# Two mixture-of-experts layers on one core: an order of experts chosen on chip, with two blocks each for the last two

## The reference

```python
grp = argmax(x @ w_group + b_group)
e_logits = (x @ w_router + b_router).reshape(t, 4, 8)[grp]
top_p, top_i = lax.top_k(softmax(e_logits), 2)
eid = grp * 8 + top_i                         # 1024 assignments
y = (silu(xs @ w1[e]) * (xs @ w3[e])) @ w2[e] # for the tokens xs of each expert e
out = sum over a token's two experts of y * its weight
```

## Time and profile before

| what | value |
|---|---|
| median of 3 runs | 2249.36 us (2246.14 to 2252.11) |
| the profiled execution | 2244.45 us, its span 2242.6 us |
| granted TensorE clock, mean | 0.959 |
| busy PE, DVE, ACT, POOL | 88%, 36%, 18%, 6% |
| moved by DMA | 440.67 MB |

### The profile page before, as it was taken

One profiled execution on the slowest core, in us unless ns is written; L12 is line 12 of the kernel. 1 busy time (PEld: TensorE's weight loads), 2 busy tenths in 40 slices (PEclk: granted clock), 3 DMA queues, 4 the chain that ended last, 5 costly groups with the idle time before them and its releaser, 6 DMA issues. The chain is left out here.

```text
span 2242.6 us, 22709 instructions
## 1 busy us (share of the span) xinstructions
PE 1968.3 (88%) x8452; PEld 1080.9 (48%) x8452; DVE 800.1 (36%) x1497; ACT 392.8 (18%) x676; POOL 135.3 (6%) x136
## 2 busy tenths in 40 slices
PE   7999998877784999999999999999988977877782
PEld 4553335544443565666557776666554322322220
DVE  3426524312115355555554554323243111111015
ACT  2335531000002123222211011111020000000000
POOL 0001010311110000000000000000002101101000
PEclk9999998999997999999999999999989999999996
DMA  8402103699977211111011115222339999999993
GB/s 230 153 33 88 56 1 151 244 420 418 418 324 226 66 47 56 47 56 43 19 65 65 64 46 159 75 75 75 131 132 391 425 427 425 421 422 424 421 404 118
DMA packets 169830, 440.67 MB, mean 197 GB/s; under 512 B 25549, under 2 KB 129741, under 8 KB 143660
## 3 DMA queue, kind: packets, MB, share of 16 engines
q1 hardware_dynamic: 159084, 423.81, 49.5%
q0 software_dynamic: 10560, 16.08, 2.0%
q10 hardware_dynamic: 128, 0.02, 0.0%
HBM read 434.21 MB, written 24.22 MB: 204 GB/s over the span
## 5 line engine op out<-in xcount | busy, mean ns | idle before, releaser
L1431 PE MATMUL bank<-stream,work 128*64 128x256 f32 (+1 forms) x1072 | 385.2, 516 | 92.9 <-DMA stream<-in_w 57.9
L1432 PE MATMUL bank<-stream,work 128*64 128x256 f32 (+1 forms) x1072 | 385.6, 516 | 0.3 <-issue 0.3
L1431 PEld LDWEIGHTS bank<-stream,work 128*64 128x64 f32 x1072 | 149.8, 144 | 284.8 <-issue 147.6
L1592 PE MATMUL bank<-hT,stream 128*128 128x512 f32 x512 | 230.4, 593 | 1.7 <-DVE hT L1016 1.7
L1444 PE MATMUL bank<-stream,work 128*64 128x512 f32 x736 | 167.1, 601 | 41.1 <-DVE work L1538 41.1
L1535 DVE TENSOR_TENSOR work<-bank,work 64x256 f32<-64x256 f32 (+1 forms) x68 | 37.8, 556 | 448.7 <-ACT work L1490 442.3
L1432 PEld LDWEIGHTS bank<-stream,work 128*64 128x64 f32 x1072 | 149.8, 144 | 34.8 <-issue 29.5
L1592 PEld LDWEIGHTS bank<-hT,stream 128*128 128x128 f32 x512 | 93.4, 190 | 99.9 <-issue 98.0
L1490 ACT ACTIVATE work<-bank 64x256 f32<-64x256 f32 (+1 forms) x68 | 33.0, 485 | 506.9 <-PE bank L1432 482.1
L1444 PEld LDWEIGHTS bank<-stream,work 128*64 128x64 f32 x736 | 54.9, 138 | 130.4 <-issue 104.4
L1914 PE MATMUL bank<-stream 128*128 128x256 f32 x480 | 111.4, 379 | 3.3 <-ACT work L1939 3.3
(11 more groups left out here) (377 smaller groups left out, 2585.2 us busy)
## 6 DMA issues: line engine op xcount, KB each, us to landing
stream<-in_w SPq DMA_DIRECT2D x99, 2048.0 KB, 19.4
stream<-in_w_in SPq DMA_DIRECT2D x68, 512.0 KB, 4.2
stream<-in_w_gate SPq DMA_DIRECT2D x34, 1024.0 KB
stream<-in_w_up SPq DMA_DIRECT2D x34, 1024.0 KB
stream<-in_w_down SPq DMA_DIRECT2D x26, 1024.0 KB
stream<-in_w_in SPq DMA_DIRECT2D x16, 1024.0 KB, 5.4
stream<-in_w_out SPq DMA_DIRECT2D x2, 4096.0 KB, 16.1
work<-in_w_down SPq DMA_DIRECT2D x8, 1024.0 KB
```

The costliest lines, as they stand in the source:

```text
L1431: pe.matmul(bank[2 + s][other:other + 64, 0:m.ff], tokens, m.wg[slot][:, k, :], start=k == 0, stop=k == KD - 1)
L1432: last = pe.matmul(bank[2 + s][mine:mine + 64, 0:m.ff], tokens, m.wu[slot][:, k, :], start=k == 0, stop=k == KD - 1)
L1592: last = pe.matmul(bank[4 + c % 2][:, :], w_hg[:, c, k, :], hT[:, k, :], start=k == 0, stop=k == KD - 1)
```

## The change

`FIXED` = 6: experts 0 to 5 keep their places. Of the other 26 the two with most tokens are found on chip. They go last, and each has two blocks (`room` = 128 tokens) that use one set of weights. The other 24 move up, so there are now 17 main pairs: pairs 0 to 14 with two experts each, pair 15 with both blocks of one of the two, pair 16 with both blocks of the other (the one with most). Spare blocks remain for what still has no room, among it whatever experts 0 to 5 have over 64. SyncE reads the expert of each place from a list that VectorE has written (`blk_i`).

```diff
+FIXED = 6
+BLOCKS = EXPERTS + 2 + SPARE
+PAIRS_MAIN, PAIRS_SPARE = EXPERTS // 2 + 1, SPARE // 2
...
             def slots(m, i, q, b, early):
+                if early is not None and early >= EXPERTS // 2 - 1:
+                    one = ((early - 13, EXPERTS // 4) if m.layer == 1 else
+                           ((1, EXPERTS // 2 - 1), (0, EXPERTS // 2))[early - EXPERTS // 2 + 1])
+                    return one, one
...
+            some = slice(FIXED, EXPERTS)
+            step(dve.scalar_tensor_tensor(m.one[:, some], m.cnt[:, some], float(SLOTS), m.r_key[:, some], ALU.mult, ALU.add))
+            for n in (1, 0):
+                step(dve.tensor_reduce(m.top[:, n:n + 1], m.one[:, some], AX_X, ALU.max))
+                step(dve.tensor_tensor(m.last[:, n, some], m.one[:, some],
+                                       m.top[:, n:n + 1].to_broadcast([P, EXPERTS - FIXED]), ALU.is_equal))
...
-            step(dve.memset(m.one, 1.0))
+            step(dve.tensor_tensor(m.nov, m.nov, m.both, ALU.max))
+            step(dve.tensor_tensor(m.nov, m.nov, m.both, ALU.subtract))
...
-            step(dve.tensor_scalar(m.t1, rank, float(SLOTS), None, ALU.is_ge))
+            step(dve.tensor_tensor(m.t1, rank, rows(m.room, EXPERTS), ALU.is_ge))
...
-            dve.tensor_copy(m.blk_i[:, 0:SPARE + 1], m.blk[:, 0:SPARE + 1]).then_inc(routed, 1)
+            for n in range(2):
+                step(dve.tensor_tensor(m.one, m.last[:, n, :], m.r_first, ALU.mult))
+                step(dve.tensor_reduce(m.top[:, 2 + n:3 + n], m.one, AX_X, ALU.add))
...
+            step(dve.tensor_scalar(m.blk[:, SPARE + 1:], m.both, 1.0 / SLOTS, None, ALU.mult))
+            dve.tensor_copy(m.blk_i, m.blk).then_inc(routed, 1)
...
-            body(PAIRS_MAIN - 2, PAIRS_MAIN // 2 - 1, 0, None, False)
-            body(PAIRS_MAIN - 1, PAIRS_MAIN // 2 - 1, 1, None, True)
+            body(EXPERTS // 2 - 2, EXPERTS // 4 - 1, 0, None, False)
+            body(EXPERTS // 2 - 1, EXPERTS // 4 - 1, 1, EXPERTS // 2 - 1, False)
+            body(EXPERTS // 2, EXPERTS // 4, 0, EXPERTS // 2, True)
...
+            def place(p):
+                return lambda: listed_expert(p + SPARE + 1)
...
             def body(i, q, b, early, last):
+                leaves = [(i * 2 + s + 1, slot) for s, (slot, _) in enumerate(m.slots(i, q, b, early))]
+                ends = [(PAIRS_MAIN * 2 - 2 + 2 * s, slot) for s, slot in enumerate((2, 3) if m.layer == 1 else (1, 0))]
...
+                elif last:
+                    next_spare(2 if m.layer == 1 else 0, ends)
+                elif m.layer == 1 and not early and q is EXPERTS // 4 - 1:
+                    next_spare(0, leaves)
+                elif early != EXPERTS // 2 - 1:
+                    reload([(n, place((i + ahead) * 2 + s), slot) for s, (n, slot) in enumerate(leaves)])
```

More of the change, by code:

```diff
@@ L1071, in __init__ @@
                 m.x_wide = m.x_rows.rearrange("p a (k q) -> p a q k", k=KD)
+                m.both, m.start, m.room, m.last, m.top = (m.h[:, a * EXPERTS:b * EXPERTS] for a, b in itertools.pairwise((0, 1, 2, 3, 5, 6)))
+                m.last = m.last.rearrange("p (a e) -> p a e", a=2)
                 m.place.append(places(m.yg[:, NT, 0:D // 2] if layer == 1 else m.sg))
@@ L1323, in reload, with listed_expert @@
                     load_gate_up(sp, m, e, slot)
-                for s, e, slot in moves:
-                    e = e()
-                    sp.wait_ge(m.d_done, i * 2 + s + 1)
+                for n, e, slot in moves:
+                    sp.wait_ge(m.d_done, n)
                     load_down(sp, m, e, slot)
-            def spare_expert(b):
-                return sp.value_load(m.blk_i[0:1, bass.ds(b, 1)], min_val=0, max_val=EXPERTS - 1)
-            def next_spare(i, places):
-                first = (i + ahead) * 2 - EXPERTS
+            def listed_expert(n):
+                return sp.value_load(m.blk_i[0:1, bass.ds(n, 1)], min_val=0, max_val=EXPERTS - 1)
@@ L1334, in next_spare @@
+            def place(p):
+                return lambda: listed_expert(p + SPARE + 1)
+            def next_spare(first, free):
                 with sp.If(need > first):
-                    reload(i, [(s, lambda s=s: spare_expert(first + s), slot) for s, slot in enumerate(places)])
+                    reload([(n, lambda s=s: listed_expert(first + s), slot) for s, (n, slot) in enumerate(free)])
             def body(i, q, b, early, last):
-                places = [slot for slot, _ in m.slots(i, q, b, early)]
@@ L1339, in body @@
-                if m.layer == 2 and early == 0:
-                    reload(i, [(0, lambda: 3, 0), (1, lambda: 4, 1)])
+                leaves = [(i * 2 + s + 1, slot) for s, (slot, _) in enumerate(m.slots(i, q, b, early))]
+                ends = [(PAIRS_MAIN * 2 - 2 + 2 * s, slot) for s, slot in enumerate((2, 3) if m.layer == 1 else (1, 0))]
+                if early == 0:
+                    reload([(n, lambda e=e: e, slot) for e, (n, slot) in enumerate(leaves, 4 if m.layer == 1 else 3)])
                 elif m.layer == 2 and early == 1:
-                    reload(i, [(1, lambda: 5, 0)])
-                elif last or ahead == 2 and not early and q is PAIRS_MAIN // 2 - 1:
-                    next_spare(i, places)
-                else:
-                    reload(i, [(s, lambda s=s: (i + ahead) * 2 + s, slot) for s, slot in enumerate(places)])
+                    reload([(4, lambda: 5, 0)])
+                elif last:
[4 more added lines that the diff above has]
+                    reload([(n, place((i + ahead) * 2 + s), slot) for s, (n, slot) in enumerate(leaves)])
```

62 lines of the change are left out of this document (42 added, 20 removed).

## The result

| | before | after |
|---|---|---|
| median | 2247.96 us (4 runs, 2246.14 to 2252.11) | 2264.00 us (4 runs, 2263.48 to 2268.82) |
| profiled execution, its span | 2244.45, 2242.6 us | 2264.08, 2262.3 us |
| clock, moved by DMA | 0.959, 440.67 MB | 0.959, 434.42 MB |

The ratio is 1.0074 (95%: 1.0061 to 1.0088): 16.6 us slower (13.7 to 19.8). The forecast was +19.5 us, 2268.9, in a range of 2258 to 2277.

The account below looks back on a forecast made before the run. Weight loads were taken to bound the middle of both layers, TensorE the first layer's end, both in turn the second's. Terms 3.6 - 3.2 + 2.9 + 16.2 = +19.5 us on 2249.36 gave 2268.9 us, range 2258 to 2277.

Parts of the forecast that it names:

- Which experts overflow: Experts 8 and 9 in layer 1, 2 and 7 in layer 2; fixed expert 2 keeps layer 2's spare pair, 34 experts loaded.
- the first rival: Second layer's end: no spare pair left, it ends after pair 16; -7.0 us in sum, 2242.4 us; chance 0.04.
- Start of the second layer, +2.9: Second layer's routing: 6.6 us of added VectorE steps less 3.7 of slack delay the first tokens by 2.9 us.
- Start of the first layer, +3.6: First layer's routing: 6.6 us of added VectorE steps less 3.0 of slack delay the first tokens by 3.6 us.
- nothing takes the delay up: Start of each layer: DMA queue runs dry, so the later first reload delays the layer's end in full, 3.6 and 2.9 us.
- something else may hold it there: Start of each layer: first reload hangs on something else, so longer routing costs nothing; +13.0, 2262.4 us; chance 0.09.
- Its end, -3.2: First layer's end: pair 16 has its tokens turned ahead, unlike the spare pair, so 16.1 us becomes 12.9.
- The bytes rival: First layer's end goes by bytes: 6.3 MB fewer save 15 us, not 3.2; +7.7, 2257.1 us; chance 0.05.
- End of the second layer, +16.2: After pair 14, three pairs bound by TensorE at 24.2 us plus 2.3 take 74.9 us against 58.7.
- List reads, nothing: SyncE's reads of two places in nearly every turn stay hidden; nothing taken, at most 1 us.
- The starts cost more: Start of each layer: slack isn't slack or TensorE's clock falls (some 1.9 us); 2270.8 to 2279.4 us; chance 0.10.
- The price that spoke for less: Routing steps: Trainium skill's 58 cycles plus columns, 94 ns each; 30 steps would be 2.8 us, hidden by slack.

Follow-up runs that it names:

- e5: Kernel before with 90 more small VectorE steps in layer 1's routing only, three times what the change adds there: 2259.03 us, ratio 1.0052.
- e3: Kernel before with 17 and 13 added VectorE steps of 32 columns in both layers, results unused: 2252.63 us, ratio 1.0027.
- e1: The change in the first layer alone, second layer as in the kernel before: 2244.94 us, ratio 0.9989 against the kernel before.
- e2: The change in the second layer alone, first layer as in the kernel before: 2265.20 us, ratio 1.0079 against the kernel before.
- e9: Kernel before with ScalarE's read of the token list moved behind the first pair's two silus: 2246.86 us, ratio 1.0005.
- e6: Kernel before without the second layer's spare pair, rows over 64 of experts 2 and 7 left out: 2213.43 us, ratio 0.9856.
- e12: Changed kernel with the unneeded block of layer 2's spare pair loading only part of its weights, 5.2 MB fewer: 2265.01 us, ratio 1.0078 against the kernel before.

## Why the prediction was right, and which terms were off

- **Which experts overflow: right.** 102 loads, a spare pair still there, and without it the time that the first rival's mechanism gives (forecast 2242.4 on a base of 2249.36, so -7.0; measured -7.4, with 7 more steps in it, and -8.8).
- **Start of the second layer, +2.9: right.** TensorE's first product came 2.9 us later (15.2 us from the counts against 12.3), and pair 14 ended 3.7 us later (mean of four new 461.3, of five old 457.6). The saturated stream passes a delay on: with three times the steps it ended 16.4 us later, where 16.1 was worked out.
- **Start of the first layer, +3.6: too high.** Means at pair 13: 233.1 against 231.5, +1.6. The step that failed is "nothing takes the delay up". The tokens and the first product did come 3.6 us later, but the first reload, which was held by something else before, went out only 1.3 to 1.5 us later in three of five new traces and 3.8 in two (at 414.79 in the changed kernel, where the sign said 418). So the rival "something else may hold it there" is half true in this layer. And pair 4 waited 2.6 us for weights before, where part of a late start is given back (e5). Yet the steps alone (e3) had pair 13 at 235.4, the whole delay, so how much is taken up varies from trace to trace.
- **Its end, -3.2: slightly low.** Pair 13 to the last pair went from 47.7 to 43.8 us, -3.9. The bytes rival (+7.7 in sum) is out: 6.3 MB fewer bought nothing more. Both together make -2.4 by the traces' means and -2.5 by e1's median (e1's own trace: -1.3), where +0.4 was forecast.
- **End of the second layer, +16.2: right in mechanism, 2.1 low by the traces.** Three traces have 79.4, 78.0 and 76.1 us, four old ones 58.5 to 60.6: +18.3 between the means. The pace of 24.2 held (23.8 to 25.6 where no fall of the clock lay in a pair). What the term left out is about 1 us of waiting for pair 15's weights and up to two falls of the clock of 1.7 us. One reading under it was wrong: the last two pairs before did not wait 3.9 and 4.1 us for weights. In that trace they waited 2.4 and 1.9 us, and the rest was a fall of the clock in each. The sum does not hang on it, since the 58.7 us were taken as measured.
- **List reads, nothing: right.** 54 reads of 0.27 us in the median, and between 2031 and 2062 us the DMA engines stay full (share 1.01), as in the earlier trace rows.
- **"The starts cost more" by a fall of the clock: the fall came** wherever a layer had the new routing and nothing else was done about it, in both layers. Its 1.9 us and more did not show in the sum: in the first layer the whole term came out too high, in the second the first reload went out 4.4 to 5.4 us later than in the kernel before (four traces), and 3.7 us of it reached pair 14.
- **The sum.** +0.4 + 19.1 = 19.5 was forecast; e1 and e2 measured -2.5 and +17.8. The whole change has +16.6 (13.7 to 19.8), so 19.5 is inside what was measured; only the first layer's +0.4 is outside its interval (-4.9 to -0.2). By the traces the layers are at -2.4 and +21.9, in sum 19.5: that this meets the forecast, and that the profiled execution is at 2264.08 where 2264 was forecast, is luck in part, since the first layer's 2.8 us too much and the second's 2.8 too little cancel. Why the traces of the second layer give some 22 us where the medians give 17.8 (14.8 to 20.9) stays open.
- **The price that spoke for less: out.** New steps stand 0.23 us apart, and 30 of them in each layer cost 6.1 us (3.6 to 8.3, e3). The tabulated price in the Trainium skill (VectorE: DVE Perf Modes, the section on the TRN2 errata), by which the steps would hide in the slack, does not hold here.

## What to carry to other kernels

When spare capacity is run in whole units, count after the change which units are still needed, from the data: moving most of an overflow away saves nothing while one unit of it stays, and here the added unit cost 25 us beside the 30 that remained. What longer work at a stage's start costs is read not from its first result but from when the stream of loads behind it starts: look for what else holds the first load back, and for the first pair that waits for its weights. A slower clock that costs nothing where pairs wait for weights costs its full time once they no longer do. And where a change depends on which items are heavy, let the fixed places go to items that are light in practice: exchanging two labels turned +17 us into -7.

## What the runs showed of the hardware

- At the start of the first layer the clock fell where TensorE waited 4.4 to 5.5 us ahead of the first products (seven traces), and not where it waited under 2 us (five); filling the wait moved the fall rather than removing it. At the start of the second layer it is the same: it fell in the traces with the old routing too where the wait was 3.5 and 3.7 us (e1, 0.72 over 1697 to 1703; e9), and stayed at 1.00 where it was 1.5 to 1.9 us (the kernel before, over 1695 to 1701; e5; e6).
- The clock also falls in spells without such a wait: 0.84 over 2182 to 2193 in the changed kernel, where TensorE had stood for 1.4 and 0.8 us between products just before. e12 has the same two gaps, and 1.00. What decides there stays open. A fall in a group of 32 products of 128x512 costs 1.6 to 1.7 us (8.78 and 8.66 against 7.09 and 7.10).
- A pair that waits for weights hid such a fall: the old spare pair of the second layer took 30.6 us at a mean clock of 0.94 (the kernel before) and at 1.00 (e1), pair 15 28.1 and 27.9.
- GpSimd's last scatter into the list (token numbers) had landed about 1 us after its end with quiet DMA queues (410.34 + 0.96, read at 412.49), and over 3 us after it where megabyte loads started meanwhile (413.30 + 0.96, read at 417.74). ScalarE's first silu stood behind that read and started at 419.64.
- Skipping 5.2 MB of loads near the end of the second layer, where DMA ran dry before (share 0.00 for 7 us), was worth nothing (1.0078 against 1.0074).
